# A two-layer model with routed experts on one core: the router's selection and gather rearranged over the engines

## The reference

```python
def hier_moe(x, wg, bg, we, be, w1, w3, w2):
    g_logits = (xt @ wg + bg).astype(jnp.float32)             # 8 groups
    g_prob = jax.nn.softmax(g_logits, axis=-1)
    g_top = jnp.argmax(g_logits, axis=-1)
    g_gate = jnp.take_along_axis(g_prob, g_top[:, None], axis=-1)
    e_logits = (xt @ we + be).astype(jnp.float32).reshape(T, N_GROUPS, EXPERTS_PER_GROUP)
    e_logits = jnp.take_along_axis(e_logits, g_top[:, None, None], axis=1)[:, 0]
    e_val, e_loc = lax.top_k(e_logits, TOPK_IN_GROUP)         # 2 of 8 experts
    gate = jax.nn.softmax(e_val, axis=-1) * g_gate
    e_id = g_top[:, None] * EXPERTS_PER_GROUP + e_loc
    ...
        h = jax.nn.silu(xb @ w1[e]) * (xb @ w3[e])            # each of 64 experts, its tokens
        return h @ w2[e]
    ...
    out = jnp.zeros_like(xt).at[row_tok].add(ys * row_w[:, None].astype(ys.dtype))
```

## Time and profile before

| | |
|---|---|
| median of 3 executions | 3058.54 us (3057.65 to 3058.82) |
| the profiled execution | 3051.9 us, span 3050.1 us |
| busy share: TensorE, VectorE, ScalarE, GpSimd | 89%, 36%, 23%, 6% |
| mean granted clock of TensorE | 0.971 of full speed |
| mean DMA rate over the span | 195 GB/s |
| rate during the expert stages | 422 GB/s |

### The profile page before, as it was taken

The page is one execution under the profiler, slowest core; times in us unless marked ns, Lnnn a source line. Parts: engine busy times, 40 slices in busy tenths (PEclk is TensorE's granted clock), DMA queues, the critical chain, the costliest instruction groups (busy, mean ns, idle before and its releaser), DMA issues.

```text
span 3050.1 us, 51036 instructions
## 1 busy us (share of the span) xinstructions
PE 2700.7 (89%) x20889; PEld 2064.3 (68%) x20889; DVE 1088.2 (36%) x2208; ACT 700.3 (23%) x1213; POOL 170.5 (6%) x209
## 2 busy tenths in 40 slices
PE   6999999999899999997778887898988967877887
PEld 6888884755578888776566666664466745666666
DVE  4555542222442234446311111146355552111114
ACT  3121331044232234222200000022065330000001
POOL 0100001000000000000000000302000001000002
PEclk8999999999999999998899999998999979999999
DMA  7655432311223223231199999942200018999993
GB/s 236 191 173 179 151 117 93 97 56 56 70 83 97 96 90 104 79 101 56 72 422 422 422 422 422 416 149 103 81 15 15 17 80 360 422 422 422 422 422 144
DMA packets 206765, 594.29 MB, mean 195 GB/s; under 512 B 9472, under 2 KB 133584, under 8 KB 157264
## 3 DMA queue, kind: packets, MB, share of 16 engines
q1 hardware_dynamic: 202880, 575.47, 49.2%
q0 software_dynamic: 3504, 16.63, 1.7%
q10 hardware_dynamic: 288, 0.89, 0.1%
HBM read 590.79 MB, written 7.41 MB: 196 GB/s over the span
## 4 chain that ended last, share of the span: by engine, by line
PE 68%; DMA 21%; DVE 6%; issue 2%; ACT 1%; SPq 1%; DVEq 0%; ACTq 0%
PE bank L1743 29%; DMA ring<-in_exp_w 21%; PE bank L2103 8%; PE bank L2186 5%; PE bank L1833 4%; PE bank L1956 4%; PE bank L1925 3%; PE bank L2077 2%; PE bank L2155 2%; PE bank L1914 1%; PE bank L2275 1%; PE bank L2004 1%; PE bank L1687 1%; SPq L472 1%; DMA ring<-in_w_ada 1%
## 5 line engine op out<-in xcount | busy, mean ns | idle before, releaser
L1743 PE MATMUL bank<-parts 128*128 128x512 f32 x2624 | 816.9, 393 | 22.5 <-DVE parts L1067 10.3
L2103 PE MATMUL bank<-ring,arena 128*64 128x256 f32 x4096 | 495.8, 392 | 179.4 <-DMA ring<-in_exp_w 178.8
L1743 PEld LDWEIGHTS bank<-parts 128*128 128x128 f32 x2624 | 492.8, 189 | 125.0 <-issue 22.4
L2103 PEld LDWEIGHTS bank<-ring,arena 128*64 128x64 f32 x4096 | 329.2, 135 | 309.5 <-issue 202.8
L1743 PE MATMUL bank<-parts,ring_low 128*128 128x512 f32 x1312 | 512.9, 391 | 0.0
L1061 DVE TENSOR_TENSOR ring_low<-ring,parts 128x2048 fp32r<-128x2048 f32 x96 | 215.2, 2245 | 204.4 <-ACT parts L689 204.1
L1743 PEld LDWEIGHTS bank<-parts,ring_low 128*128 128x128 f32 x1312 | 247.9, 189 | 52.3
L1513 DVE SCALAR_TENSOR_TENSOR arena<-arena,bank 128x128 f32<-128x128 f32 x128 | 44.2, 345 | 656.3 <-ACT arena L826 656.3
L2121 PEld LDWEIGHTS bank<-arena,ring 128*64 128x64 f32 x8192 | 266.0, 138 | 16.5 <-ACT arena L667 1.1
L2121 PE MATMUL bank<-arena,ring 128*64 128x64 f32 x8192 | 263.3, 222 | 0.7 <-ACT arena L667 0.7
L689 ACT ACTIVATE parts<-ring 128x2048 fp32r<-128x2048 f32 x96 | 179.8, 1873 | 237.6 <-DMA ring<-in_w_ffn_in 110.9
(11 more groups left out here) (316 smaller groups left out, 2670.7 us busy)
## 6 DMA issues: line engine op xcount, KB each, us to landing
ring<-in_exp_w SPq DMA_DIRECT2D x384, 1024.0 KB, 10.3
ring<-in_w_ffn_in SPq DMA_DIRECT2D x44, 1024.0 KB, 5.5
ring<-in_w_ada SPq DMA_DIRECT2D x36, 1024.0 KB, 5.5
ring<-in_w_ffn_out SPq DMA_DIRECT2D x20, 1024.0 KB, 5.1
ring<-in_w_in SPq DMA_DIRECT2D x18, 1024.0 KB, 5.1
ring<-in_conv_w_in SPq DMA_DIRECT2D x12, 1024.0 KB, 5.2
ring<-in_attn_w_in SPq DMA_DIRECT2D x10, 1024.0 KB, 9.4
ring<-in_attn_w_out SPq DMA_DIRECT2D x8, 1024.0 KB, 5.1
```

Source lines behind the costliest of these rows:

```text
L1743: i = mm(o, a[:, cols[0], cols[1]], b, start=first_ and n == 0, stop=last_ and n == 2)
L2103: x = mm(bank[s][64 * f:64 * f + 64, 0:2 * P].rearrange("p (w n) -> p w n", w=2), XW[:, s, k], ring[:, 3 * s:3 * s + 2, c0:c0 + 2 * P - 1: ...
```

## The change

- VectorE's router does one operation for four tiles: the logits of all tiles go to one bank, group and experts are found with comparisons, products and reductions over three-dimensional views (some of them repeated by a stride of zero).
- BEFORE, ONES and EA are rounded copies, so that the rank products are rounded products. ScalarE makes BEFORE and ONES.
- The rests XTL are made by GpSimd. XTL moves to the place beside XTH, SEL gets memory of its own.
- FIRST and SEL are made in two halves of 512 slots, the FIRST of the next tile ahead of the SEL of this one. The plan comes behind them, the gate weights behind the plan.
- The gather of the first half goes tile by tile over all eight banks, that of the second by channel tile. The weight row comes behind the gather.
- The first experts are taken out of the loops. Between `up(2)` and the loop stand the turning of the weight row and of SEL, with VectorE's copies. GpSimd's row loads stand behind that turning.
- YST is cleared in two parts, behind the gather and behind the weight row.

The diff, cut to its core ("..." marks what is left out; in stretches that are rewritten only the new lines stand):

```diff
-        XTL = sb("xt_low", [P, TT, D], F32R)
+        SEL = sb("picked", [P, TT, PAIRS], F32R)
...
-        SEL = rounded(4096, TT, PAIRS)
+        XTL = rounded(8192, TT, D)
         SEL32 = SEL.bitcast(F32)
-        FIRST = rounded(17408, TT, PAIRS)
+        FIRST = rounded(4096, TT, PAIRS)
         FIRST32 = FIRST.bitcast(F32)
         YST = area(0, KT, SLOTS)
-        XST = area(8704, KT, SLOTS)
-        SWT = rounded(17408, 8, SEQ)
-        YSH = (rounded(8704, 8, 512), rounded(0, 8, 512))
-        YSL = (rounded(12800, 8, 512), rounded(21504, 8, 512))
+        YFLAT = area(0, KT * SLOTS)
...
+        BEFORE = rounded(21504, 1, P)[:, 0]
+        ONES = rounded(21632, 1, P)[:, 0]
...
+                for t in range(TT):
+
+                    pool.wait_ge(sem("xt"), 4 * layer + t + 1)
+                    pool.tensor_tensor(grouped(XTL, t), byrow(t), grouped(XTH, t).bitcast(F32), ALU.subtract)\
+                        .then_inc(sem("xt_low"), 1)
                 pool.wait_ge(sem("moe_xst"), 16 * layer + 16)
-                for n, v in enumerate((layer, 2 + layer) + ((5, 7) if layer else ())):
-                    pool.dma_start(ROWS[:, n], lnrows[v].partition_broadcast(P)).then_inc(sem("ln_vectors"), 16)
...
+                for s in range(2):
+                    pool.wait_ge(a_b, s + 1)
+                    window(2 + s, s)
+
+                pool.wait_ge(sem("moe_swtp"), 8 * layer + 8)
+                for v, row in enumerate((layer, 2 + layer) + ((5, 7) if layer else ())):
+                    pool.dma_start(ROWS[:, v], lnrows[row].partition_broadcast(P)).then_inc(sem("ln_vectors"), 16)
+                with pool.Fori(2, n) as i:
...
+                A_(BEFORE, before, ACT.Copy).then_inc(sem("moe_ge"), 1)
+                A_(ONES, ones[:], ACT.Copy).then_inc(sem("moe_ge"), 1)
...
+                act.wait_ge(sem("moe_wrow"), l + 1)
+                for c in range(2):
+                    evac(WROW[0:2, c], bank[2 + c][0:2, :], "moe_wrow_out")
...
+                def leading(values, top, hot):
+
+                    seq(TTn(tie, values, over_8(top), ALU.is_equal))
+                    seq(TTn(tie, tie, back4, ALU.mult))
+                    seq(nc.vector.tensor_reduce(first_of, tie, AXX, ALU.max))
+                    seq(TTn(hot, back4, over_8(first_of), ALU.is_equal))
...
+                dve.wait_ge(sem("moe_logits"), 4 * l + 4)
                 st.wait()
+                seq(TTn(LG, bank[0][:, 0:4 * 72].rearrange("p (t n) -> p t n", t=TT),
+                        rbias[:, l].unsqueeze(1).broadcast_to([P, TT, 72]), ALU.add))
+                groups, choice = LG[:, :, 0:GROUPS], LG[:, :, GROUPS:72]
+                seq(nc.vector.tensor_reduce(best, groups, AXX, ALU.max))
+                TSc(negm, best, -1.0, None, ALU.mult).then_inc(sem("moe_m"), 1)
+                leading(groups, best, oh)
+                seq(TTn(pairs(tmp), pairs(choice), over_e(oh), ALU.mult))
+                seq(nc.vector.tensor_reduce(el, tmp.rearrange("p t (g e) -> p t e g", g=GROUPS), AXX, ALU.add))
+                seq(nc.vector.tensor_reduce(best1, el, AXX, ALU.max))
+                leading(el, best1, oh1)
+                seq(STT(out=rest8, in0=oh1, scalar=TAKEN, in1=el, op0=ALU.mult, op1=ALU.add))
+                seq(nc.vector.tensor_reduce(best2, rest8, AXX, ALU.max))
+                leading(rest8, best2, oh2)
+                seq(TTn(oh12, oh1, oh2, ALU.add))
+                TTn(pairs(EA), over_e(oh), over_g(oh12), ALU.mult).then_inc(sem("moe_ea"), 1)
+                TTn(dif, best2, best1, ALU.subtract).then_inc(sem("moe_m"), 1)
+                st.did(TTn(pairs(E0), over_e(oh), over_g(oh1), ALU.mult))
+                st.did(TTn(pairs(E1), over_e(oh), over_g(oh2), ALU.mult))
+                nc.vector.memset(XST[:, :, PAIRS:SLOTS], 0.0).then_inc(sem("moe_tail"), 1)
 
+                dve.wait_ge(sem("moe_rank"), l + 1)
+                seq(nc.vector.tensor_copy(cnt, bank[5][:, 256:320]))
+                seq(nc.vector.tensor_tensor_scan(cum, one64, cnt, 0.0, ALU.mult, ALU.add))
+                seq(TTn(startf, cum, cnt, ALU.subtract))
+                seq(TTn(RN, bank[5][:, 0:256].rearrange("p (t n) -> p t n", t=TT),
+                        startf.unsqueeze(1).broadcast_to([P, TT, 64]), ALU.add))
+                st.did(TTn(tmp, E0, RN, ALU.mult))
+                seq(TTn(E1, E1, RN, ALU.mult))
+                st.did(nc.vector.tensor_reduce(d0, tmp, AXX, ALU.add))
+                seq(nc.vector.tensor_reduce(d1, E1, AXX, ALU.add))
+
+                for c in range(2):
+                    S = slice(512 * c, 512 * c + 512)
+                    made = []
+                    for t in range(TT + 1):
+                        if t < TT:
+                            st.did(TSc(FIRST[:, t, S], slotrow[:, S], d0[:, t:t + 1], None, ALU.is_equal))
+                            made.append(st.n)
+                        if t:
+                            dve.wait_ge(sem("dve_step"), made[t - 1])
+                            STT(out=SEL[:, t - 1, S], in0=slotrow[:, S], scalar=d1[:, t - 1:t], in1=FIRST32[:, t - 1, S],
+                                op0=ALU.is_equal, op1=ALU.add).then_inc(sem("moe_sel"), 1)
+                for j in range(MAX_ROUNDS):
...
+                dve.wait_ge(sem("moe_gather"), 16 * l + 16)
+                st.did(nc.vector.memset(YFLAT[:, 0:4096], 0.0))
+                dve.wait_ge(sem("moe_wrow"), l + 1)
                 st.wait()
+                nc.vector.memset(YFLAT[:, 4096:KT * SLOTS], 0.0).then_inc(sem(f"moe{l}_add"), 1)
...
+                hidden(1, 1)
+                collect(0, 0)
+                hidden(2, 0)
+                dve.wait_ge(sem("moe_wcol"), l + 1)
+                st.did(nc.vector.tensor_copy(WSLOT[:, 0:16], bank[6][:, 0:16]))
+                for g in range(8):
+                    dve.wait_ge(sem("moe_swtp"), 8 * l + g + 1)
+                    nc.vector.tensor_copy(SWT[g], bank[(1, 3, 7)[g % 3]][:]).then_inc(sem("moe_swt"), 1)
+                st.wait()
+                TTn(WSLOT[:, 16:24], WSLOT[:, 0:16:2], WSLOT[:, 1:16:2], ALU.add).then_inc(sem("moe_wslot"), 1)
+                collect(1, 1)
+                with dve.Fori(2, n) as i:
...
-                    x = mm(bank[t][:, 0:72], U[:, k, P * t:P * t + P], rw[:, l, k], start=(k == 0), stop=(k == KT - 1))
+                    x = mm(bank[0][:, 72 * t:72 * t + 72], U[:, k, P * t:P * t + P], rw[:, l, k],
+                           start=(k == 0), stop=(k == KT - 1))
...
+                pe.wait_ge(sem("moe_ge"), 7 * l + 2)
                 pe.wait_ge(sem("moe_ea"), l + 1)
                 for t in range(TT):
                     for j in range(t + 1):
+                        mm(bank[5][:, 64 * t:64 * t + 64], BEFORE if j == t else ONES, EA[:, j],
                            start=(j == 0), stop=(j == t))
                 for j in range(TT):
+                    x = mm(bank[5][:, 256:320], ONES, EA[:, j], start=(j == 0), stop=(j == 3))
                 x.then_inc(sem("moe_rank"), 1)
 
+                def gather(c, k, t):
+                    for j, part in enumerate((XTH, XTL)):
+                        x = mm(bank[k][:], part[:, t, P * k:P * k + P], SEL[:, t, 512 * c:512 * c + 512],
+                               start=(t == j == 0), stop=(t == TT - 1 and j == 1))
+                    if t == TT - 1:
+                        x.then_inc(sem("moe_gather"), 1)
+
+                for t in range(TT):
+                    pe.wait_ge(sem("moe_sel"), 8 * l + t + 1)
+                    pe.wait_ge(sem("xt_low"), 4 * l + t + 1)
+                    for k in range(KT):
+                        gather(0, k, t)
+                pe.wait_ge(sem("moe_sel"), 8 * l + 8)
+                for k in range(KT):
+                    pe.wait_ge(sem("moe_xst"), 16 * l + k + 1)
+                    for t in range(TT):
+                        gather(1, k, t)
                 pe.wait_ge(sem("moe_wsplit"), 2 * l + 2)
+                pe.wait_ge(sem("moe_xst"), 16 * l + 12)
+                for c in range(2):
+                    for t in range(TT):
                         for j, picked in enumerate((FIRST, SEL)):
+                            x = mm(bank[2 + c][0:2, :], WH[:, TT * j + t], picked[:, t, 512 * c:512 * c + 512],
                                    start=(t == j == 0), stop=(t == TT - 1 and j == 1))
                 x.then_inc(sem("moe_wrow"), 1)
...
+                up(1, 16, 1)
+                pe.wait_ge(sem("moe_wrow_out"), 2 * l + 2)
+                for s in range(2):
+                    turn(s, s)
+                    down(s, 16, s)
+                up(2, 32, 0)
+                for s in range(8):
+                    x = tp(bank[6][:, 2 * s:2 * s + 2], WROW[0:2, s // 4, P * (s % 4):P * (s % 4) + P], ident[0:2, 0:2])
+                x.then_inc(sem("moe_wcol"), 1)
+                for g in range(8):
+                    if g >= 3:
+                        pe.wait_ge(sem("moe_swt"), 8 * l + g - 2)
```

(34 more changed lines are left out.)

140 lines of the change are left out of this document (23 added, 117 removed).

## The result

The changed kernel takes **3013.69 us** (median of 4 executions, 3011.37 to 3015.11); the kernel before, beside it, 3058.51 us. The ratio is 0.9855 (95% interval 0.9841 to 0.9868), so it is 44.8 us faster. On another chip the same pair had 3015.63 and 3054.39 us, ratio 0.987 (0.9853 to 0.9888), 38.8 us. The sum had said 38.7 and 3019.8.

The account below looks back on a forecast made before the run. The first expert product's end was taken to set the start of a DMA-bound load stream; 20.3 us (layer 0) and 18.4 (layer 1) make 38.7, so 3058.5 - 38.7 = 3019.8 us, range 3004 to 3037.

Parts of the forecast that it names:

- The sum: Whole kernel: 20.3 us gained in layer 0 and 18.4 in layer 1, together 38.7 us, giving a median of 3019.8 us.
- part 7: Expert load stream from U0 to the last load: 467.0 us in layer 0, 469.0 in layer 1, against 468.6 before.
- Part 1: Router on VectorE, logits to EA: new steps take 4.85 us; undisturbed, EA would end 6.5 us earlier.
- Part 2: Rests by GpSimd: 3.2 us per operation, VectorE held behind two of them, EA only 2.2 us earlier than before.
- Part 3: Rounded rank products: 14 instructions, 3.2 us in place of 6.2, then 2.8 us of further steps.
- Part 4: Selection in halves, plan (3.3 us) behind it: the gather waits 1.45 us in place of 7.95.
- Part 5: Gather: 29.44 us plus 2.4 for the low clock, 31.85 in all, ending 17.4 us earlier.
- Part 6: Behind the gather, with the weight row moved there: U0 comes 8.0 us after the gather's end, 18.7 us earlier than before.
- U0: End of the first expert product, which lets the load of expert 2 start; forecast at 1486.6 us against 1505.31.
- A: Rival in the router: GpSimd holds only `negm`, two-input operations run freely; EA 3.2 us earlier per layer, 3013.4 us; chance 0.20.
- B: Rival in the stream: SEL's turning and unhidden row loads starve it, 11.7 us more, 3031.5 us; chance 0.22.
- C: Rival in the router: GpSimd's strided difference far dearer, VectorE waits; at 14 us each the kernel takes 3063; chance 0.05.

Follow-up runs that it names:

- e1: Changed kernel with the rests of tiles 2 and 3 made by VectorE between the selection's halves, not by GpSimd: 3008.2 us.
- a0_after: The changed kernel itself, run and profiled again without any edit: 3015.63 us.
- e5: Changed kernel with the plan (rounds, starts and counters) ahead of the selection again: 3018.8 us.
- e4: Changed kernel with TensorE waiting for the SEL of all four tiles of the first half before the gather's first product: 3021.0 us.
- e8: Changed kernel with nine products of no use between the rank products and the gather: 3011.5 us.
- e10: As e9, with 14 products of no use ahead of the ranks and 16 ahead of the gather in place of 11 and 9: 2998.84 us.
- e9: Changed kernel with the edits of e1, e7 and e8 together, and 11 products of no use ahead of the ranks too: 3001.6 us.
- e7: Changed kernel with two of layer 1's four row loads issued behind the expert loop: 3008.9 us.

## Why the prediction was right, point by point

The path was right: each step up to the first product came out within 0.7 us in layer 0. The stream (part 7) came out near its number for a reason that was partly luck, told below.

- **What bounds**: right. The first product's end moved, and the whole stream with it.
- **Part 1, chain to EA**: the steps took 0.22 us each; EA ended 9.4 us behind the last logit in layer 0 (said: 9.9). The reduction over the strided view took 0.61 us in place of the 0.45 in the sum, within the 0.2 left to the range.
- **Part 2, GpSimd**: 2.84 us an operation beside VectorE and 2.92 to 3.04 alone (said: 3.2 between 2.36 and 3.9). VectorE is held, also with two SBUF inputs: e1 shows it, which the rows of before could not. The Trainium skill's rule (page "SBUF — State Buffer", section "Who interferes with whom": two SBUF inputs against a GpSimd operation that reads SBUF exclude each other for a whole instruction) agrees with 2.72 against 0.19 us, and its exemption of reductions with the 0.19 us of L1431. In layer 1 only one operation was held, because the logits came later, and the hold was shorter than said; in a0_after's layer 1 two were held. So the hold's mechanism was forecast, but whether a layer pays 2.3 us for it or 3.5 to 3.7 was not forecast and changes from one execution to the next.
- **Part 3, ranks**: 3.3 us (said: 3.2); then 2.84 us to the slots (said: 2.8).
- **Part 4, selection and plan**: 1.6 us to the first SEL (said: 1.45). The plan's move was put at 3.3 and showed 3.6 us in e5. A later tile took 1.06 us, so e4 showed 2.8 us where 3 x 1.06 is 3.2: a small miss.
- **Part 5, gather**: 32.5 and 31.65 us (said: 31.85), start 17.3 and 16.0 us behind the last logit (said: 17.4). The low clock was there as forecast; e8 shows 2.3 and 1.3 us of it. Without it the new order of products takes 30.0 to 30.1 us (e8, e10) and not the 29.44 of the sum.
- **Part 6**: first product 7.5 us behind the gather where I had 8.0, since the 0.42 us of issue were covered. U0 was put 57.2 us behind the last logit; it is 57.3 and 55.2.
- **Part 7, stream**: turning ended and product 3 followed as computed:

```profile
1497.85 3.79 PE L2107 MATMUL bank<-ring,arena 128*64 128x256 f32 x32
...
1507.97 0.32 PE L2114 MATMUL bank<-keep,arena 128*128 128x128 f32 x1 [1.32 <-DVE parts L1528]
1508.22 3.85 PE L2107 MATMUL bank<-ring,arena 128*64 128x256 f32 x32
...
1489.01 106.01 SPq L476 DMA_DIRECT2D ring<-in_exp_w  x44
```

Product 2 (L2107) starts 8.8 us behind U0, product 3 ends at 23.1 (said: 23.6). The stream took 465.1 us in layer 0 (said: 467.0) and 468.7 in layer 1 (said: 469.0). The standstill of the expert loads behind the turning was there. From 1511 to 1514 (first two rows), 22 to 25 us behind U0, the rows' queue (q0) moved 0.95 MB and that of the experts (q1) 0.25; in layer 1 four row loads held the engines until about 2515 (next two, from 2509 to 2515), though product 3 had ended at 2509.78:

```profile
q0 software_dynamic: 259, 0.95, 77.1%
q1 hardware_dynamic: 46, 0.25, 22.7%
...
q0 software_dynamic: 469, 1.75, 84.7%
q1 hardware_dynamic: 53, 0.31, 14.0%
...
1945.10 7.77 SPq L476 DMA_DIRECT2D ring<-in_exp_w  x2
```

The sum itself has an error. The load that ends the stretch (issued at 1943.61, landed at 1954.12) is the 184th of the layer's 186; two are issued behind it (last row). So 186 x 2.486 is 5.0 us too much, and 0.6, 184 x 2.486 and 3.7, with the 0.3 for a late start, make 462.0 in layer 0 and 464.0 in layer 1. Against that the stream lost 3.1 and 4.7 us more than the sum had for its start, its standstill and its rows. One such term is the first load, which landed 4.9 us behind its issue, where 0.6 and 2.486 are 3.1. Two errors of opposite sign left 1.9 and 0.3 us: that part of the hit is luck. Counted right and with nothing else changed, the forecast would have been 9.9 us lower, about 3010 us.
- **Sum**: 42.7 us in the two stretches in place of 38.7, a difference of 4.0, of which 1.9 is the stream in layer 0, 0.3 that in layer 1 and 1.8 the earlier first product in layer 1. That the medians then moved by 44.8 in one batch and 38.8 in the next is the executions' spread.
- **Rivals**: A would have given 3013.4 us, nearly the number measured in the first batch, and is wrong all the same: its mechanism (two-input operations run freely) is ruled out by the rows above. B is wrong as a whole, since the stream got 3.5 us shorter in layer 0 and no longer in layer 1; a part of it, row loads that aren't hidden, is there in layer 1. C was never near at 2.84 us.

## What to carry to other kernels

Where a DMA-bound stage waits for one event, count the distance to that event, and move behind it whatever the stream can hide; of the parts that were undone one by one that was the largest. (The router in one operation for four tiles, the selection in halves as a whole and the late weight row were not undone; what they gave is read from the rows.) Work given to GpSimd isn't free if VectorE's own chain runs at the same time: put it where VectorE idles or reduces, or let VectorE do it between two pieces that are ahead of their reader. A number that fits a rival doesn't prove it: look for the row that its mechanism needs. Nor does a sum that comes out prove its terms: count the loads up to the very row that ends the stretch.

## What was not expected of the hardware

TensorE kept the high clock over some idle times and not over others: over 0.87 us ahead of e8's gather, over 2.56 us ahead of e9's ranks, but it had lost it behind the 2.37 us ahead of e9's gather. In layer 1 of e9 it fell between 2430 and 2431, about 1 us after TensorE had taken up work behind 1.95 us of idle time, and in e10 in the midst of products (0.66 from 1440 to 1441, 0.50 to 1443), although TensorE's last idle time, 1.93 us, had ended at 1437.72. What decides is left open.

Layer 1's stream takes 2.2 to 4.4 us longer than layer 0's in the variants of the changed kernel (468.7 against 465.1 in the first) and 0.7 in e7, while the kernel before has 468.6 and 468.7 (469.0 and 469.7 again). In the first profile the difference stands almost whole at the tenth load, which landed 32.69 us behind the first issue in layer 0 and 36.10 in layer 1:

```profile
1512.70 9.00 DMA ring<-in_exp_w
...
2510.41 12.39 DMA ring<-in_exp_w
```

It arises while the row loads run, but with two of the four taken away the tenth load of layer 1 still landed at 35.14 (e7). So a share of 1 to 2 us is the rows', and the rest is open. Loading the rows during the gather was not tried, because SEL lies in their place.
